# Seven pairs of experts instead of six in a mixture, with a pair last whose outputs come back through the matrix engine

## The chip, the cores and the metric

The kernel runs on one core of a Trainium2 chip as one launch. The metric is the device time of that launch in microseconds. The engines are TensorE (PE in the profile: matmuls; PEld: its weight loads), VectorE (DVE), ScalarE (ACT), GpSimd (POOL), and SyncE (SP), whose queue issues most of the transfers.

## The reference, cut to what matters

Two transformer blocks run one after the other on 512 tokens of width 1024, in float32. The first ends in a mixture of 32 experts, of which the router picks 4 for each token, and a gated addition of a second input `p`. That part is:

```python
def expert_block(args):
    xblk, e = args
    hg, hl = jnp.split(xblk @ w_gu[e] + b_gu[e], 2, axis=-1)
    hg = jnp.minimum(hg, SWIGLU_LIMIT)
    hl = jnp.clip(hl, -SWIGLU_LIMIT, SWIGLU_LIMIT)
    glu = hg * jax.nn.sigmoid(hg * SWIGLU_ALPHA)
    return ((hl + 1.0) * glu) @ w_down[e] + b_down[e]
...
y = (yb * row_gate[:, None]).astype(x2d.dtype)
return jnp.zeros((t + 1, d), x2d.dtype).at[row_tok].add(y)[:t]
...
h = DEEPNORM_ALPHA * x + ffn
h = h + jax.nn.sigmoid(h @ ple_gate_w[i]) * (p[i] @ ple_proj[i])
x = _layer_norm(h, ln2_g[i], ln2_b[i])
```

An expert's weights are 1024x2048 and 1024x1024 floats, 12.6 MB; the 32 of them are 403 MB, all of which is read.

## The kernel before, in words

The mixture is one stage, in which each engine runs its own instruction stream and they meet at semaphores. Its work is cut into **units**. A **single** is one expert with up to 128 tokens: its weights are split into two reduced-precision halves (`wh` on ScalarE, `wl` on VectorE), and each product is three matmuls (`wide_chunk`, L2632 to L2634). A **pair** is two experts with up to 64 tokens each, side by side in the 128 columns of the array, with plain float32 matmuls and no split (`pair_chunk`, L2651 and L2652). Experts are ranked by their number of tokens; the first `FEW` = 2 x `PAIRS` ranks, the smallest, go to the pairs. Tokens beyond an expert's room are counted in `over`; if there are any, `RestOfExperts` computes every expert again for the late tokens, with all 512 columns.

An expert's weights are 12 **chunks** of 1 MB (`CHUNKS`; a pair has 24). SP issues them in order (`chunk_in`, L2452) into 8 slots (`raw` and two in a borrowed tile, shown as `y` in the DMA rows); a pair has 8 more slots, `more_raw`, which lie over `wh` and `wl`. An issue waits until its slot is free: `w_low` counts chunks split, `used` chunks multiplied. The order of units is `s s p s s s p ... s s s`, 20 singles and 6 pairs: each turn of the loop in `all_units` is a single, a pair and two singles.

Around a unit, GpSimd gathers the rows of the next unit's tokens (L2511) and scatters the finished unit's outputs with addition into `y_rows` in memory (L2516), after ScalarE has weighted them by the gates (`weighted`, L2743). `kept` and `returned` order these.

After the last unit comes `Embedding` (`ple`). TensorE computes `p @ ple_proj` in 8 tiles (`embedded_tile`, L3166 to L3168, 48 matmuls), which needs `p` and the projection split by ScalarE (L3218, L3222) and VectorE (`vector_p` L3253, `vector_proj` L3257). Then `turn` (L3179) transposes the sums that SP has read back from `y_rows` (`sync_y`, L3152) once the last scatter has landed; VectorE adds them to `x` (L3270), and ScalarE and VectorE split `x` (L3240, L3273). Dummy matmuls stand between the transposes (`K.keep_busy`, L236). Then come 8 gate tiles (`tile`, L3192 to L3197, 24 matmuls each), each followed by a sigmoid on ScalarE (L3245), and the layer norm.

## Time and profile before

| | |
|---|---|
| time, median of 3 runs | 3280.78 us (3277.88 to 3282.35) |
| span of the profiled execution, first to last instruction | 3281.2 us |
| TensorE busy | 3121.0 us, 95% |
| VectorE, ScalarE, GpSimd busy | 2092.6, 1598.0, 211.7 us |
| moved by transfers | 600.37 MB, 183 GB/s over the whole span |

The page gives the span and no other time for the profiled execution, so sums are made against 3281.2 us, which lies 0.4 us above the median of the runs. Times in the rows are counted from the start of the span. The mixture stage reaches from about 477 to 1557 us. Matmuls overlap: a 128x512 matmul is shown as 0.39 us long while the next starts 0.23 us later, so the distance of the starts is what counts.

### The profile page before, as it was taken

How to read it: one execution, taken by the hardware profiler on the slowest of the kernel's cores; microseconds unless marked ns; L12 is line 12 of the kernel's file. 1: busy time of each engine (PE TensorE's matmuls, PEld its weight loads, DVE VectorE, ACT ScalarE, POOL GpSimd, SP SyncE). 2: the span in 40 equal slices, each digit the busy share in tenths (PEclk: the TensorE clock that was granted, in tenths of full speed). 3: DMA queues.
4: the chain of work that ended last, by engine and by line, in shares of the span. 5: the costliest groups of instructions: out<-in, count | busy, mean ns of one | idle time of the engine just before them, and what ended most of it. 6: DMA issues, size and time to landing. Idle time of an engine off the chain costs nothing. (4 is left out here: it accounts for less than half of the span.)

```text
span 3281.2 us, 48141 instructions
## 1 busy us (share of the span) xinstructions
PE 3121.0 (95%) x18751; PEld 2346.5 (72%) x18751; DVE 2092.6 (64%) x2561; ACT 1598.0 (49%) x1943; POOL 211.7 (6%) x202
## 2 busy tenths in 40 slices
PE   8998899999989999999999999999999999999998
PEld 6876567574747474848768777788877776778886
DVE  6745758484848484849478866666438876566544
ACT  4424336464646473737376355444226536444422
POOL 0000001121212121211000000000000000000000
PEclk9999999999999999999999999999999999999999
DMA  4113259999999999998122111222322211123331
GB/s 152 59 33 104 79 198 373 412 399 410 390 407 387 409 388 403 392 406 322 63 87 72 66 46 40 89 97 97 108 73 78 72 65 37 54 87 99 96 106 62
DMA packets 117708, 600.37 MB, mean 183 GB/s; under 512 B 19490, under 2 KB 23090, under 8 KB 67138
## 3 DMA queue, kind: packets, MB, share of 16 engines
q1 hardware_dynamic: 105442, 580.57, 46.6%
q0 software_dynamic: 12096, 17.40, 2.1%
q8 instruction: 122, 2.00, 0.2%
q14 instruction: 48, 0.39, 0.0%
HBM read 582.62 MB, written 27.33 MB: 186 GB/s over the span
## 5 line engine op out<-in xcount | busy, mean ns | idle before, releaser
L2823 DVE TENSOR_TENSOR wl<-raw,wh 128x2048 fp32r<-128x2048 f32 x174 | 397.1, 2288 | 69.8 <-ACT wh L2736 68.9
L2736 ACT ACTIVATE wh<-raw 128x2048 fp32r<-128x2048 f32 x174 | 333.5, 1917 | 134.3 <-PE pu L2634 62.4
L4740 ACT ACTIVATE w_high<-w_raw 128x1024 fp32r<-128x1024 f32 (+1 forms) x112 | 129.0, 1152 | 302.0 <-PE acc L4712 161.1
L2632 PE MATMUL pu<-wh,Xh 128*128 128x512 f32 x640 | 259.8, 406 | 16.2 <-DVE wl L2823 16.2
L4789 DVE TENSOR_TENSOR w_low<-w_raw,w_high 128x1024 fp32r<-128x1024 f32 (+1 forms) x112 | 150.0, 1339 | 180.4 <-PE ps L4670 95.1
L2633 PE MATMUL pu<-wl,Xh 128*128 128x512 f32 x640 | 253.1, 395 | 0.0
L2634 PE MATMUL pu<-wh,Xl 128*128 128x512 f32 x640 | 253.0, 395 | 0.0
L4692 PE MATMUL ps<-x_high,w_high 128*128 128x512 f32 x640 | 249.1, 389 | 0.0
L4693 PE MATMUL ps<-x_low,w_high 128*128 128x512 f32 x640 | 249.0, 389 | 0.0
L3537 PE MATMUL acc<-x_high,w_high 128*128 128x512 f32 x528 | 219.7, 416 | 1.5 <-ACT hq L3946 1.5
L3538 PE MATMUL acc<-x_low,w_high 128*128 128x512 f32 x528 | 207.5, 393 | 1.7 <-issue 1.7
L4670 PE MATMUL ps<-x_high,w_low 128*128 128x512 f32 x704 | 173.2, 389 | 0.5 <-DVE w_low L4789 0.5
L2632 PEld LDWEIGHTS pu<-wh,Xh 128*128 128x128 f32 x640 | 122.4, 191 | 45.7 <-DVE wl L2823 18.1
L2823 DVE TENSOR_TENSOR wl<-y,wh 128x2048 fp32r<-128x2048 f32 x66 | 150.9, 2287 | 3.3 <-ACT wh L2736 3.3
L4670 PEld LDWEIGHTS ps<-x_high,w_low 128*128 128x128 f32 x704 | 132.0, 188 | 28.7 <-DVE w_low L4789 1.4
L4214 DVE TENSOR_TENSOR w_low<-w_raw,w_high 128x1024 fp32r<-128x1024 f32 (+1 forms) x102 | 115.8, 1138 | 51.8 <-PE acc L3543 23.5
L2634 PEld LDWEIGHTS pu<-wh,Xl 128*128 128x128 f32 x640 | 122.4, 191 | 27.2
L2633 PEld LDWEIGHTS pu<-wl,Xh 128*128 128x128 f32 x640 | 122.7, 192 | 24.1
L4705 PE MATMUL acc<-h_high,w_high 128*128 128x512 f32 x352 | 137.2, 390 | 1.5 <-DVE h_low L4823 1.5
L4692 PEld LDWEIGHTS ps<-x_high,w_high 128*128 128x128 f32 x640 | 120.2, 188 | 25.4 <-DVE cv L4800 0.4
L4693 PEld LDWEIGHTS ps<-x_low,w_high 128*128 128x128 f32 x640 | 120.1, 188 | 24.9
L2736 ACT ACTIVATE wh<-y 128x2048 fp32r<-128x2048 f32 x66 | 126.8, 1922 | 21.7 <-DMA y<-in_exp_w 8.7
(920 smaller groups left out, 7208.9 us busy)
## 6 DMA issues: line engine op xcount, KB each, us to landing
raw<-in_exp_w SPq DMA_DIRECT2D x234, 1024.0 KB, 16.1
y<-in_exp_w SPq DMA_DIRECT2D x78, 1024.0 KB
more_raw<-in_exp_w SPq DMA_DIRECT2D x72, 1024.0 KB, 17.4
w_raw<-in_w_in SPq DMA_DIRECT2D x100, 512.0 KB, 3.4
w_raw<-in_w_up SPq DMA_DIRECT2D x80, 512.0 KB, 3.7
w_raw<-in_w_down SPq DMA_DIRECT2D x32, 704.0 KB, 4.0
w_raw<-in_w_out SPq DMA_DIRECT2D x32, 384.0 KB, 3.1
kv_raw<-in_w_mem_kv SPq DMA_DIRECT2D x16, 512.0 KB, 3.8
```

The costliest lines, as they stand in the source:

```text
L2632: nc.tensor.matmul(o, lh[:, k, :], wh[:, m % PARTS, c], start=(m >= 8 and kh == 0 and kk == 0), stop=False)
L2633: nc.tensor.matmul(o, lh[:, k, :], wl[:, m % PARTS, c], start=False, stop=False)
L2634: mm = nc.tensor.matmul(o, ll[:, k, :], wh[:, m % PARTS, c], start=False, stop=end)
L2736: nc.scalar.activation(wh[:, m % PARTS, :], piece, ACT.Copy).then_inc(w_high, 1)
L2823: nc.vector.tensor_tensor(wl[:, m % PARTS, :], slot_of(n, m)[0], wh[:, m % PARTS, :], ALU.subtract).then_inc(w_low, 1)
L3537: nc.tensor.matmul(o, wh[:, n % 3, c], high[:, k, :], start=(k == 0), stop=False)
L3538: nc.tensor.matmul(o, wh[:, n % 3, c], low[:, k, :], start=False, stop=False)
L4670: mm = nc.tensor.matmul(o, wl[:, u % 2, c], high[:, k, :], start=False, stop=(k == DT - 1))
L4692: nc.tensor.matmul(o, wh(u)[:, c], high[:, k, :], start=(k == 0), stop=False)
L4693: nc.tensor.matmul(o, wh(u)[:, c], low[:, k, :], start=False, stop=False)
L4705: nc.tensor.matmul(o, wh(u)[:, c], hh[:, f * PART + k, :], start=(f == 0 and k == 0), stop=False)
L4789: nc.vector.tensor_tensor(wl[:, u % 2, 0:width(u)], raw_of(u), wh(u), ALU.subtract).then_inc(low_ready, 1)
```

## The change

There are 7 pairs and 18 singles in the order `sssp` four times and `ssp` three times, so that the last unit is a pair (`ORDER`; `Unit` now works its counts out from its place). The last unit's outputs are not scattered to memory. ScalarE weights them into `y_parts`, rounded to reduced precision, and VectorE makes the remainder (`weighted_low`). VectorE also makes a matrix of zeros and ones that says to which token each row belongs (`place_back`). TensorE multiplies the two parts by it (`join`, 16 matmuls), which gives the outputs in the layout of `x`, and VectorE adds them (`take_joined`). The transposes of `y_rows` are moved ahead of `embedded_tile` and alternate with the joins, and the dummy matmuls between them are gone. SP reads `y_rows` when six chunks of the last pair are used and all earlier scatters have landed, before the projection and `p`. The splits of `p` and the projection on VectorE now come after the additions; the splits of `x` go beside `embedded_tile`. GpSimd's work after the last unit is gone. ScalarE weights the unit before a pair two places earlier. Four small memsets (`tile_starts`) are added at the stage's start.

```diff
-PAIRS = 6
+PAIRS = 7
 FEW, WIDE = 2 * PAIRS, EXPERTS - 2 * PAIRS
 UNITS = WIDE + PAIRS
 HALF = SLOTS // 2
+SCATTERS = WIDE + 2 * (PAIRS - 1)
+ORDER = 4 * "sssp" + 3 * "ssp"
+ROUND_FROM, ROUNDS, ROUND_UNITS, ROUND_WIDE, ROUND_PAIRS = 4, 3, 4, 3, 1
...
-        unit(a3, a4)
-    unit(Unit(UNITS - 1, WIDE - 1, EXPERTS - 2, one + (3 * one + two) * PAIRS + one, 1, PAIRS, PAIRS, 12, last=True), None)
+    def run(places, i=0):
+        for place in places:
+            unit(Unit(place, i), Unit(place + 1, i) if place + 1 < UNITS else None)
+
+    run(range(ROUND_FROM))
+    with eng.Fori(0, ROUNDS) as i:
+        run(range(ROUND_FROM, ROUND_FROM + ROUND_UNITS), i)
+    run(range(ROUND_FROM + ROUNDS * ROUND_UNITS, UNITS))
 
 
...
                 sp.wait_ge(saved, 16)
-                sp.wait_ge(w_low, (WIDE - 1) * CHUNKS + 7)
+                sp.wait_ge(scattered, SCATTERS * 16)
+                sp.wait_ge(used, (UNITS - 1) * CHUNKS + 6)
+                ple.sync_y(sp)
+                sp.wait_ge(used, (UNITS - 1) * CHUNKS + 10)
                 ple.sync_proj(sp)
-                sp.wait_ge(w_low, (WIDE - 1) * CHUNKS + 8)
                 ple.sync_p(sp)
-                rest.sync(sp, used)
-                sp.wait_ge(used, (UNITS - 1) * CHUNKS + 8)
-                for n in range(3):
-                    ple.sync_gate(sp, n)
-                sp.wait_ge(scattered, (UNITS + PAIRS) * 16)
-                ple.sync_y(sp)
-                for n in range(3, DT):
+                rest.sync(sp, joined_taken, DT)
+                for n in range(DT):
                     ple.sync_gate(sp, n)
 
             @block.gpsimd
@@ -2556,9 +2565,6 @@
                 pool.wait_ge(cleared, 2)
                 pool.wait_ge(kept, 16 * NT)
                 all_units(pool, unit)
-                scatter(Unit(UNITS, WIDE, 0, 0, 0, PAIRS, 0, 0))
-                pool.wait_ge(scattered, (UNITS + PAIRS) * 16)
-                pool.sem_inc(returned, 1)
 
             @block.tensor
             def _(pe):
...
+
+                def join(odd, k):
+
+                    if k == 0:
+                        pe.wait_ge(back_placed, 1)
+                        pe.wait_ge(y_low, 2)
+                    if k >= 2:
+                        pe.wait_ge(joined_taken, k - 1)
+                    c = slice(k * P, (k + 1) * P)
+                    nc.tensor.matmul(pd[:, k % 2, :], y_parts[:, odd, c], back_sel, start=True, stop=False)
+                    nc.tensor.matmul(pd[:, k % 2, :], y_parts[:, 1 - odd, c], back_sel, start=False, stop=True).then_inc(joined, 1)
 
...
-                rest.tensor(pe, y_ready)
+                for k in range(DT):
+                    ple.tensor_turn(pe, k)
+                    join((UNITS - 1) % 2, k)
+                rest.tensor(pe)
                 ple.tensor(pe)
 
...
-                def weighted(at, odd, d):
+                def weighted(at, odd, d, split):
                     act.wait_ge(used, at * CHUNKS + (11 + d))
                     if d == 0:
                         act.wait_ge(returned, at + 1)
                         act.wait_ge(paid, at * 2 + 2)
-                    nc.scalar.activation(y[:, odd, d * 512:(d + 1) * 512], pd[:, d, :], ACT.Copy, scale=gneg[:, odd:odd + 1]).then_inc(y_ready, 1)
+                    to = y_parts if split else y
+                    nc.scalar.activation(to[:, odd, d * 512:(d + 1) * 512], pd[:, d, :], ACT.Copy, scale=gneg[:, odd:odd + 1]).then_inc(y_ready, 1)
 
                 def gate(n, c):
                     act.wait_ge(used, n.at * CHUNKS + (4 * c + 2))
@@ -2773,16 +2794,17 @@
                                 turned_part(n.at - 1, 1, False)
                                 x_part(n, 0)
                                 x_part(n, 1)
-                            if m in (2, 3):
-                                weighted(n.at - 1, 1 - n.odd, m - 2)
+                            if m in ((0, 1) if n.pair else (2, 3)):
+                                weighted(n.at - 1, 1 - n.odd, m % 2, False)
                         if m in (5, 9):
                             gate(n, (m - 5) // 4)
                         if m == 8:
                             turned_part(n.at, 0, n.pair)
                     if n.pair:
...
-                        x_part(following, 0)
-                        x_part(following, 1)
+                        if not n.last:
+                            x_part(following, 0)
+                            x_part(following, 1)
 
                 nc.scalar.activation(rl[:, :].rearrange("p (j g e) -> p j g e", j=NT, g=4),
...
-                turned_part(UNITS - 1, 1, False)
+                for d in (0, 1):
+                    weighted(UNITS - 1, (UNITS - 1) % 2, d, True)
                 ple.scalar_p(act)
-                act.wait_ge(w_low, (WIDE - 1) * CHUNKS + 10)
                 ple.scalar_proj(act)
-                for d in (0, 1):
-                    weighted(UNITS - 1, 1, d)
+                act.wait_ge(joined_taken, DT)
                 rest.scalar(act)
...
+
+                def place_back(n):
+
+                    nc.vector.tensor_copy(back_row[:, 0:1], back[:, n.odd:n.odd + 1]).then_inc(back_rows, 1)
+                    dve.wait_ge(back_rows, 1)
+                    nc.vector.tensor_scalar(back_row[:, 1:1 + NT], tile_starts[:, :], back_row[:, 0:1], None, ALU.add).then_inc(back_rows, 1)
+                    dve.wait_ge(turned, n.at * 2 + 2)
+                    dve.wait_ge(back_rows, 2)
+                    nc.vector.tensor_tensor(back_sel.rearrange("p (j s) -> p j s", j=NT), K.c("iota").unsqueeze(1).to_broadcast([P, NT, P]),
+                                            back_row[:, 1:1 + NT].unsqueeze(2).to_broadcast([P, NT, P]), ALU.is_equal).then_inc(back_placed, 1)
+
+                def weighted_low(at, odd, d):
+                    c = slice(d * 512, (d + 1) * 512)
+                    if d == 0:
+                        dve.wait_ge(scattered, SCATTERS * 16)
+                    dve.wait_ge(y_ready, at * 2 + (d + 1))
+                    nc.vector.scalar_tensor_tensor(y_parts[:, 1 - odd, c], pd[:, d, :], gneg[:, odd:odd + 1], y_parts.bitcast(F32)[:, odd, c],
+                                                   ALU.mult, ALU.subtract).then_inc(y_low, 1)
+
+                def take_joined(k):
+                    dve.wait_ge(joined, k + 1)
+                    nc.vector.tensor_tensor(x[:, k, :], x[:, k, :], pd[:, k % 2, :], ALU.add).then_inc(joined_taken, 1)
 
                 def pay(at, odd, pair=False):
...
                             turned_low(n.wide, 0)
-                    if not n.last and not n.pair:
+                    if n.last:
+                        place_back(n)
+                    elif not n.pair:
...
+                for j in range(NT):
+                    step.go(nc.vector.memset(tile_starts[:, j:j + 1], -float(j * P)))
...
-                turned_low(WIDE - 1, 1)
+                for d in (0, 1):
+                    weighted_low(UNITS - 1, (UNITS - 1) % 2, d)
+                for k in range(DT + 1):
+                    if k < DT:
+                        ple.vector_turned(dve, k)
+                    if k:
+                        dve.wait_ge(ple.added, k)
+                        take_joined(k - 1)
                 ple.vector_p(dve)
                 ple.vector_proj(dve)
-                rest.vector(dve, used)
-                dve.wait_ge(used, UNITS * CHUNKS)
+                rest.vector(dve)
                 ple.vector(dve)
 
...
+    def tensor_turn(self, pe, k):
+        if k >= 3:
+            pe.wait_ge(self.added, k - 2)
+        for j in range(NT):
+            if k == 0:
+                pe.wait_ge(self.y_in[j], 16)
+            mm = self.nc.tensor.transpose(self.bank[k % 3][:, j * P:(j + 1) * P], self.yt[:, j, k * P:(k + 1) * P], self.K.c("ident"))
+        mm.then_inc(self.turned, 1)
...
-            if k:
-                K.keep_busy(norm.spare, 256)
-            if k >= 3:
-                pe.wait_ge(self.added, k - 2)
...
+            nc.scalar.activation(self.high[:, t, :], self.x[:, t, :], ACT.Copy).then_inc(self.x_split_h, 1)
             if t in (2, 5):
                 high_part(t // 3)
-        for k in range(DT):
-            act.wait_ge(self.added, k + 1)
-            nc.scalar.activation(self.high[:, k, :], self.x[:, k, :], ACT.Copy).then_inc(self.x_split_h, 1)
         for n in range(DT):
             act.wait_ge(self.product, n + 1)
...
+    def vector_turned(self, dve, k):
+        dve.wait_ge(self.turned, k + 1)
+        self.nc.vector.tensor_tensor(self.x[:, k, :], self.x[:, k, :], self.bank[k % 3], ALU.add).then_inc(self.added, 1)
+
...
-        low_part(0)
-        low_part(1)
         for k in range(DT):
-            dve.wait_ge(self.turned, k + 1)
-            nc.vector.tensor_tensor(x[:, k, :], x[:, k, :], self.bank[k % 3], ALU.add).then_inc(self.added, 1)
-            if k:
-                dve.wait_ge(self.x_split_h, k)
-                nc.vector.tensor_tensor(low[:, k - 1, :], x[:, k - 1, :], high[:, k - 1, :], ALU.subtract).then_inc(self.x_split_l, 1)
-        dve.wait_ge(self.x_split_h, DT)
-        nc.vector.tensor_tensor(low[:, DT - 1, :], x[:, DT - 1, :], high[:, DT - 1, :], ALU.subtract).then_inc(self.x_split_l, 1)
+            dve.wait_ge(self.x_split_h, k + 1)
+            nc.vector.tensor_tensor(low[:, k, :], x[:, k, :], high[:, k, :], ALU.subtract).then_inc(self.x_split_l, 1)
+            if k in (3, 6):
+                low_part(k // 3 - 1)
         for n in range(DT):
             dve.wait_ge(self.gate, n + 1)
             dve.wait_ge(self.e_taken, n + 1)
```

## Rows read from the trace of the kernel before

**Rows 1.** The page's part 2: the span in 40 equal slices, the transfers' rate.
```profile
GB/s 152 59 33 104 79 198 373 412 399 410 390 407 387 409 388 403 392 406 322 63 87 72 66 46 40 89 97 97 108 73 78 72 65 37 54 87 99 96 106 62
```

**Rows 2.** Busy time by stretches: a pair, and the two singles after the last pair.
```profile
core 0: us, PE busy (x) PEld busy (x) DVE busy (x) ACT busy (x) POOL busy (x), PEclk, DMA share, GB/s
...
574.00:621.00 47.00, 46.58 (x231) 15.96 (x229) 6.05 (x12) 6.51 (x10) 4.83 (x6) 1.00 1.01 411
...
1446.00:1522.00 76.00, 73.22 (x338) 59.16 (x335) 72.47 (x56) 62.23 (x48) 17.00 (x13) 0.98 1.02 409
```

**Rows 3.** TensorE's timeline (start, duration in us): openings of units 0, 1, 2, 7, 15, 23, 25.
```profile
500.44 0.51 PE L2604 MATMUL pu<-brow,ones 32*128 32x512 f32 x4 [0.86 <-DVE Xl L2842]
...
538.24 0.51 PE L2604 MATMUL pu<-brow,ones 32*128 32x512 f32 x4
...
574.58 0.64 PE L2601 MATMUL pu<-brow,ones 32*64 32x512 f32 x1
...
785.16 0.51 PE L2604 MATMUL pu<-brow,ones 32*128 32x512 f32 x4
...
1115.10 0.51 PE L2604 MATMUL pu<-brow,ones 32*128 32x512 f32 x4
...
1446.52 0.50 PE L2604 MATMUL pu<-brow,ones 32*128 32x512 f32 x4
...
1522.63 0.50 PE L2604 MATMUL pu<-brow,ones 32*128 32x512 f32 x4
```

**Rows 4.** The transfers' view from 1430 to 1458 us.
```profile
DMA packets 1607, 11.72 MB, mean 419 GB/s; under 512 B 176, under 2 KB 176, under 8 KB 176
```

**Rows 5.** Line 2452, issue to landing: from 500 to 560 us, then from 1100 to 1530.
```profile
DMA to landing us min/median/max: 4.9/7.2/9.6
...
DMA to landing us min/median/max: 10.8/16.5/29.0
```

**Rows 6.** TensorE at the sixth pair's last chunk and the single behind it.
```profile
1442.93 0.61 PE L2651 MATMUL pd<-more_raw,h 128*64 128x512 f32 x1 [1.32 <-issue]
...
1450.07 0.40 PE L2633 MATMUL pu<-wl,Xh 128*128 128x512 f32 x1
1450.30 0.39 PE L2634 MATMUL pu<-wh,Xl 128*128 128x512 f32 x1
...
1453.05 0.63 PE L2632 MATMUL pu<-wh,Xh 128*128 128x512 f32 x1
1453.48 0.63 PE L2633 MATMUL pu<-wl,Xh 128*128 128x512 f32 x1
```

**Rows 7.** TensorE behind the last unit: projection, transposes, first gate tile.
```profile
1557.70 0.47 PE L3166 MATMUL pu<-p_high,v_high 128*128 128x512 f32 x1
...
1568.45 0.39 PE L3168 MATMUL pu<-p_high,v_low 128*128 128x512 f32 x1
1569.96 0.33 PE L3179 MATMUL pu<-const,y_tokens 128*128 128x128 f32 x1 [1.11 <-DMA y_tokens<-y_rows]
...
1573.78 0.48 PE L3179 MATMUL pu<-const,y_tokens 128*128 128x128 f32 x1 [0.95 <-DMA y_tokens<-y_rows]
```

**Rows 8.** ScalarE in the same stretch.
```profile
1557.71 0.69 ACT L2743 ACTIVATE y<-pd,gneg 128x512 f32<-128x512 f32 x1 [2.03 <-PE pd L2634]
...
1568.88 0.60 ACT L3235 ACTIVATE e<-pu 128x512 f32<-128x512 f32 x1 [0.68 <-PE pu L3168]
...
1588.10 0.60 ACT L3245 ACTIVATE g<-pu 128x512 f32<-128x512 f32 x1 [3.38 <-PE pu L3197]
```

**Rows 9.** VectorE in the same stretch.
```profile
1551.72 1.22 DVE L3253 TENSOR_TENSOR p_low<-p_raw,p_high 128x1024 fp32r<-128x1024 f32 x1
1553.13 2.29 DVE L3257 TENSOR_TENSOR v_low<-v_raw,v_high 128x2048 fp32r<-128x2048 f32 x1 [0.19 <-ACT v_high L3222]
...
1578.58 0.68 DVE L3270 TENSOR_TENSOR x<-x,pu 128x512 f32<-128x512 f32 x1
1579.18 0.69 DVE L3273 TENSOR_TENSOR x_low<-x,x_high 128x512 fp32r<-128x512 f32 x1
```

More of the change, by code:

```diff
@@ L2305 @@
 HALF = SLOTS // 2
+SCATTERS = WIDE + 2 * (PAIRS - 1)
+ORDER = 4 * "sssp" + 3 * "ssp"
+ROUND_FROM, ROUNDS, ROUND_UNITS, ROUND_WIDE, ROUND_PAIRS = 4, 3, 4, 3, 1
 class Unit:
-    def __init__(self, at, wide, rank, bias, odd, pairs, turn, off, pair=False, behind=False, first=False, last=False):
-        self.at, self.wide, self.rank, self.bias, self.odd, self.pairs, self.turn, self.off, self.pair = at, wide, rank, bias, odd, pairs, turn, off, pair
-        self.behind, self.first, self.last = behind, first, last
@@ L2316, in all_units, with __init__ @@
-def all_units(eng, unit):
-    one, two = 64, 128
-    unit(Unit(0, 0, EXPERTS - 1, one, 0, 0, 0, 0, first=True), Unit(1, 1, FEW, 2 * one, 1, 0, 0, 12))
-    with eng.Fori(0, PAIRS) as i:
-        u, l, b = i * 4, i * 3, i * (3 * one + two)
-        a0 = Unit(u + 1, l + 1, l + FEW, b + 2 * one, 1, i, i, 12)
-        a1 = Unit(u + 2, l + 1, i * 2, b + (2 * one + two), 0, i, i, 24, pair=True)
-        a2 = Unit(u + 3, l + 2, l + (FEW + 1), b + (3 * one + two), 1, i + 1, i, 36, behind=True)
-        a3 = Unit(u + 4, l + 3, l + (FEW + 2), b + (4 * one + two), 0, i + 1, i, 48)
-        a4 = Unit(u + 5, l + 4, l + (FEW + 3), b + (5 * one + two), 1, i + 1, i, 60)
-        unit(a0, a1)
-        unit(a1, a2)
-        unit(a2, a3)
-        unit(a3, a4)
-    unit(Unit(UNITS - 1, WIDE - 1, EXPERTS - 2, one + (3 * one + two) * PAIRS + one, 1, PAIRS, PAIRS, 12, last=True), None)
+    def __init__(self, place, i=0):
+        before = ORDER[:place]
+        singles, self.pair = before.count("s"), ORDER[place] == "p"
+        self.first, self.last = place == 0, place == UNITS - 1
+        self.behind = not self.first and ORDER[place - 1] == "p"
+        self.odd, self.off, self.turn = place % 2, place * CHUNKS, i * (16 * ROUND_UNITS * CHUNKS // RAW)
+        self.at = i * ROUND_UNITS + place
+        self.wide = i * ROUND_WIDE + (singles - self.pair)
+        self.pairs = i * ROUND_PAIRS + before.count("p")
+        self.rank = EXPERTS - 1 if self.first else i * (2 * ROUND_PAIRS) + 2 * before.count("p") if self.pair else i * ROUND_WIDE + (FEW + singles - 1)
+        self.bias = i * (64 * ROUND_WIDE + 128 * ROUND_PAIRS) + (64 * (singles + (not self.pair)) + 128 * (before.count("p") + self.pair))
@@ L2361, in mixture @@
         vc = K.sb(ctx, "vc", [P, 512])
+        with ExitStack() as high:
+            y_parts = K.sb(high, "y_parts", [P, 2, D], F32R)
         y = K.sb(ctx, "y", [P, 2, D])
@@ L2373, in mixture @@
             sg = K.sb(held, "sg", [P, 512])
+            with ExitStack() as high:
+                hb_parts = K.sb(high, "hb_parts", [P, 2, 512], F32R)
             hb = K.sb(held, "hb", [P, 2, 512])
@@ L2424, in slot_of @@
                 where = raw[:, v, :] if v < HELD else spare_raw[:, v - HELD, :]
-                return where, loaded[v], n.turn * 96 + (16 * ((n.off + c) // RAW) + 16)
+                return where, loaded[v], n.turn + (16 * ((n.off + c) // RAW) + 16)
             def pair_slot(n, c):
@@ L2793, in _ @@
                 nc.scalar.activation(gpart[:, :, :, 0], ranked, ACT.Copy).then_inc(g_high, 1)
-                start = Unit(0, 0, EXPERTS - 1, 64, 0, 0, 0, 0, first=True)
+                start = Unit(0)
                 high_part(start, 0)
@@ L3169, in embedded_tile @@
             mm.then_inc(self.e_made, 1)
-        def turn(k):
-            if k:
-                K.keep_busy(norm.spare, 256)
-            if k >= 3:
-                pe.wait_ge(self.added, k - 2)
-            for j in range(NT):
-                if k == 0:
-                    pe.wait_ge(self.y_in[j], 16)
-                mm = nc.tensor.transpose(bank[k % 3][:, j * P:(j + 1) * P], self.yt[:, j, k * P:(k + 1) * P], K.c("ident"))
-            mm.then_inc(self.turned, 1)
         def tile(n):
@@ L3201, in tensor @@
             embedded_tile(t)
-        for k in range(DT):
-            turn(k)
         for n in range(DT):
```

22 lines of the change are left out of this document (11 added, 11 removed).

## The prediction

> **What bounds the kernel now.** The slices of the page come first, because they show which resource is full in the mixture stage. From the seventh slice to the eighteenth (about 490 to 1480 us) 373 to 412 GB/s flow, and nowhere else in the kernel more than 322 [rows 1]. The busy times by stretches say whether that is the limit. In a pair's 47 us ScalarE and VectorE are nearly idle; in the two singles after a pair TensorE, VectorE and ScalarE work for 73, 72 and 62 of 76 us; in both the transfers' share is 1.0 [rows 2]. So I looked at the distance from issue to landing. A chunk takes 4.9 us when the queue is nearly empty, which happens only under the first two singles; from 1100 us on it never takes under 10.8 us [rows 5], so four chunks or more are always outstanding, and the queue doesn't run dry. With no gather or scatter in the way 419 GB/s flow [rows 4]: 1.049 MB in 2.50 us.
>
> The starts of the units give the periods. From the second pair's end to the sixth's, 785.2 to 1446.5 us, four rounds of three singles and a pair take 165.3 us each [rows 3]. Their 60 chunks need 60 x 2.50 = 150.0; the other 15.3 us go to the gathers and scatters of four units, 3.8 us each. The transfers set the round, and each pair ends when its last weights do: TensorE begins the last chunk at 1442.93 after a wait and is done 3.6 us later [rows 6, 3]. Only the start, where eight slots fill before TensorE begins at 500.4, and the end, where three singles at TensorE's own pace follow the last pair, are outside this rule. The last single ends at 1557.7, and the outputs' way through memory comes behind it [rows 3, 7].
>
> **The change part by part.** I add up to the moment at which the first gate tile's product is taken by ScalarE, 1588.1 before [rows 8]. What follows is unchanged.
>
> *The start.* Two singles up to 574.6 as before; a third directly behind singles costs what the second did, 574.6 - 538.2 = 36.3 (36.4 with the unrounded start) [rows 3]: 610.9. The stretch from the first pair's start to the second pair's end is the same sequence as before, 785.2 - 574.6 = 210.6: 821.5. Two more `sssp` rounds, as from 785.2 to 1115.1, 329.9 [rows 3]: 1151.4.
>
> *Three rounds of `ssp`.* TensorE alone needs 76.1 for the two singles behind a pair (1522.6 - 1446.5) [rows 3] and 47 for a pair that doesn't wait [rows 2], 123; the queue needs 48 x 2.50 + 3 x 3.8 = 131.4. It sets the round: 394.2, so the last pair ends at T = 1545.6. If the 15.3 us go with bytes and not with units, the round is 165.3 x 48/60 = 132.2 and T = 1548.0; if gathers and scatters cost the queue nothing, TensorE's 123 would bind and T = 1520, which the period of 165.3 for 60 chunks excludes. I take 131.4, because the rate falls in the stretches where gathers run. Pairs and singles together do not need fewer bytes: all 384 chunks are still read, and one unit's gather and scatter are saved, which has paid for the third single at the start (36.3 against 33.8). So the advance of T, 1557.7 - 1545.6 = 12.1 us, comes almost wholly from having a unit last that follows its weights by 3.6 us in place of three that lag.
>
> *Coming back.* The last chunk lands at T - 3.6 = 1542.0. The four reads of `y_rows` stand behind it in SP's queue, and nothing of SP's stands between; they wait for scatters that have long landed. They come 1.27 us apart, (1573.78 - 1569.96)/3 [rows 7]: the fourth at 1547.1. In the meantime ScalarE weights the second half in 0.69 and VectorE makes its remainder, for which the trace has no row; the nearest VectorE operations of 128x512 take 0.68 to 0.69 [rows 8, 9]: 1547.1 too. With 0.4 for the last transposes, VectorE begins to add at 1547.5. It has 16 additions, one starting 0.60 behind the other [rows 9]. TensorE's part of each step, four transposes and two matmuls, is about 1.0 against VectorE's 1.2: VectorE sets it, 9.6 plus 0.6 for the first wait: 1557.7. Below, the joins can't be free; above, if TensorE's steps set the pace at half clock, a step takes 1.9 and the loop 5.6 more.
>
> *The projection.* VectorE turns to `p_low` and `v_low` only now. Before, they were covered by the last single; now nothing covers them, 1.22 + 2.29 = 3.5 [rows 9], and TensorE waits: 1561.2. The 48 matmuls take 1568.7 - 1557.7 = 11.0 [rows 7]: 1572.2. The copy of the last tile behind them costs 0.6 (the `e` row) [rows 8], and 0.5 because ScalarE now also splits `x` and two weight tiles there, about as much work as TensorE's: 1573.3. The first gate tile has 24 matmuls at 0.227, 5.5, and 0.2 until ScalarE has it: 1579.0. The splits of `x` on VectorE run beside this and are 3 us ahead of their use. The clock comes on top.
>
> *TensorE's clock.* Behind the sixth pair TensorE is idle while a single's first chunk is split, and soon after, matmuls that had started 0.23 apart start 0.43 apart [rows 6], 1.2 in place of 2.4 GHz. The slow stretch begins after 1450.3 and reaches to about 1453.9: 3.4 us, at half rate a loss of 1.7. The new wait for `v_low`, 1557.2 to 1561.2, is as long at least, and the dummy matmuls are gone, so I take the 1.7 in full: 1580.7. The Trainium skill (TensorE: Matmul & The Clock Gate, Part 1: The HAM clock gate) says that the throttled state is the default and activity alone releases it. By that rule the removal of the dummy matmuls speaks against the change, and the sum ends at 1580.7; without it, at 1579.0.
>
> *What costs nothing.* The four memsets run while VectorE waits for a TensorE product at the start; uncovered, under 0.3. `place_back` waits for the last transposes of the pair and has three chunks' time, some 11 us, before it is needed; uncovered, 0.9. GpSimd's last scatter goes, and nobody waits for it. The earlier `weighted` frees a bank sooner within a pair. The projection and `p` land within 5 us behind `y_rows`, and their ScalarE splits lie beside the additions; if `p` were late, 3 us.
>
> Sum: 1588.1 - 1580.7 = 7.4 us off 3281.2, which is 3273.8 against the profiled execution and 3273.4 against the median; rounded, 3273.5.
>
> **The rivals.**
>
> *The small transfers go with bytes (15%).* For it: rates hardly differ between a pair's stretch and the whole round. T is 2.4 later: 3275.9. With the joins at half clock for one stretch of 3.4 us, which costs another 1 to 2, it ends at 3277: no measurable change.
>
> *The queue runs dry behind each pair (9%).* This ends on the slow side. The last four chunks of a pair are issued only when the seventh and eighth chunk are multiplied. With one single fewer between pairs TensorE arrives with less in store. If the queue empties there, each of the three `ssp` rounds pays up to one landing from an empty queue, 4.9 [rows 5]: 14.7 in all, 3288. It takes away the whole gain from 2.5 us a round, and is slower by over 0.2% from 4.7. Against it: the shortest landing in the later rounds is 10.8 [rows 5], 5.9 above the empty queue's, so that more than two chunks' lead would have to go; and TensorE already waits for its last chunk in the old pairs [rows 6].
>
> *The end is lighter (14%).* The clock holds through the new wait and the joins overlap more, and the stream is a little quicker for having one unit less: 1.7 + 2 to 3, 3269.
>
> *The pairs overflow (1%).* The change doesn't do what it says if an expert of ranks 12 and 13 has more than 64 tokens, because `RestOfExperts` then runs: 32 experts with 192 matmuls each of at least 0.39 us, over 2 ms. Against it: counting the router's choices on the reference's inputs, the fourteenth smallest of the ranked experts has 63 tokens.
>
> **How the numbers follow.** The forecast has 61%, with its own range from 3270 to 3277: T is open by 2.4 us, the clock by 1.7, the loop by some 2. A change of 0.2%, 6.6 us, is about what a measurement of this kernel can tell from none; it ends at 3274.2, inside that range. So of the forecast's 61% two thirds are faster and one third the same. Faster: 0.41 + 0.14 = 0.55. Same: 0.20 + 0.15 and a little of the dry queue = 0.36. Slower: 0.09, the dry queue and the overflow. Two in ten may be left out: the dry queue's worst and half of the lightest end, so the range goes from 3268 to 3280.
>
> **What would show it.** In the profile after, the units' starts: third single near 574.6, the first pair near 611, pairs ending near 821, 1151, 1283, 1414 and 1546, with TensorE's waits inside the late pairs grown to about 8 us. Issue to landing never under 8 us after 700. Behind the last pair, transposes from about 1546, additions on VectorE without gaps until 1558, an idle TensorE of about 4 us before `embedded_tile`, and the first sigmoid of the gate tiles near 1581. I am wrong if the last pair ends later than 1549, if the loop of the joins takes 15 us in place of 10, or if the drop of the clock comes twice.

## The result, and the profile of the changed kernel

The changed kernel takes 3267.39 us (median of 4 runs, 3265.16 to 3268.45), the kernel before 3281.57 on the same chip: ratio 0.9949, 95% interval 0.9937 to 0.9962, so 12 to 21 us faster. That is a gain of 14 us where 7.4 were forecast, and 0.6 us under the low end of the range. The profiled span went from 3281.2 to 3266.0 us.

TensorE's timeline of the changed kernel, the rows that answer to [rows 3]: the first single, the second, the third, the first pair, then the single behind the first, second, fourth, fifth and sixth pair, and the last pair's last chunk (as in [rows 6]).

```profile
504.31 0.50 PE L2610 MATMUL pu<-brow,ones 32*128 32x512 f32 x4 [0.90 <-DVE Xl L2863]
...
542.11 0.51 PE L2610 MATMUL pu<-brow,ones 32*128 32x512 f32 x4
...
577.85 0.50 PE L2610 MATMUL pu<-brow,ones 32*128 32x512 f32 x4
...
614.30 0.64 PE L2607 MATMUL pu<-brow,ones 32*64 32x512 f32 x1
...
661.00 0.50 PE L2610 MATMUL pu<-brow,ones 32*128 32x512 f32 x4
...
823.52 0.50 PE L2610 MATMUL pu<-brow,ones 32*128 32x512 f32 x4
...
1150.39 0.51 PE L2610 MATMUL pu<-brow,ones 32*128 32x512 f32 x4
...
1280.28 0.51 PE L2610 MATMUL pu<-brow,ones 32*128 32x512 f32 x4
...
1409.57 0.51 PE L2610 MATMUL pu<-brow,ones 32*128 32x512 f32 x4
...
1534.67 0.61 PE L2668 MATMUL pd<-more_raw,h 128*64 128x512 f32 x1 [1.28 <-issue]
```

The forecast's moments were 821, 1151, 1283, 1414 and 1546. Counted from the first unit (504.3 here, 500.4 before), the second pair ends 1.9 us early, the fourth 4.9, the fifth 6.4, the sixth 8.5, and the last, at 1538.2, 11.3. The three `ssp` rounds take 129.9, 129.3 and 128.6 us, not 131.4; `sssp` takes 163.4 on the mean of the two between 823.52 and 1150.39, not 165.

VectorE behind the last pair (answers to [rows 9]): first and last additions of the loop, then the two remainders.

```profile
1539.98 0.69 DVE L3306 TENSOR_TENSOR x<-x,pu 128x512 f32<-128x512 f32 x1
...
1549.41 1.28 DVE L2908 TENSOR_TENSOR x<-x,pd 128x512 f32<-128x512 f32 x2
1550.60 1.22 DVE L3298 TENSOR_TENSOR p_low<-p_raw,p_high 128x1024 fp32r<-128x1024 f32 x1
1551.74 2.28 DVE L3302 TENSOR_TENSOR v_low<-v_raw,v_high 128x2048 fp32r<-128x2048 f32 x1
```

TensorE in the same stretch (to [rows 7]): the wait for `v_low`, and where the spacing of matmuls changes.

```profile
1554.17 0.77 PE L3226 MATMUL pu<-p_high,v_high 128*128 128x512 f32 x1 [4.63 <-DVE v_low L3302]
1554.73 0.63 PE L3227 MATMUL pu<-p_low,v_high 128*128 128x512 f32 x1
1555.16 0.63 PE L3228 MATMUL pu<-p_high,v_low 128*128 128x512 f32 x1
...
1560.23 0.40 PE L3228 MATMUL pu<-p_high,v_low 128*128 128x512 f32 x1
1560.46 0.40 PE L3226 MATMUL pu<-p_high,v_high 128*128 128x512 f32 x1
```

ScalarE (to [rows 8]): the last `e` tile and the first gate tile.

```profile
1568.61 0.59 ACT L3282 ACTIVATE e<-pu 128x512 f32<-128x512 f32 x1
...
1575.06 0.60 ACT L3290 ACTIVATE g<-pu 128x512 f32<-128x512 f32 x1 [5.34 <-PE pu L3246]
```

Measured from the last pair's end T, the steps came as forecast until the projection: first addition T + 1.8 (forecast 1.9), loop done T + 12.4 (12.1), `v_low` done T + 15.8 (15.6). Then matmuls start 0.43 us apart for nearly 6 us, and the gate tile comes at T + 36.9 instead of 35.1.

So the change of the span is made up thus: mixture from 1057.3 to 1033.9, 23.4 us off; tail (T to the first gate tile) from 30.4 to 36.9, 6.5 on; what lies ahead of the first unit 3.9 on, what lies behind the gate tile 1693.1 to 1691.0, 2.1 off. The last two can't be ascribed to the change as they stand: over the twelve further executions profiled below, the start lay between 501.3 and 504.3 (501.4 to 502.6 for the three with the old order) and the rear between 1690.2 and 1699.9. On the mean of all profiled executions the start is 503.3 with the new order and 501.5 with the old, so up to 1.8 us of it may be the change's; no run separates them. Two questions were left: why the stream is 11.3 us ahead of the forecast, and what the tail costs.

The packets gave the first clue. The transfers' view of 700 to 1480 us shows that more bytes flow in the same time (before, 399 GB/s, then after):

```profile
DMA packets 49853, 311.06 MB, mean 399 GB/s; under 512 B 10190, under 2 KB 10190, under 8 KB 13489
```

```profile
DMA packets 50605, 316.33 MB, mean 406 GB/s; under 512 B 10242, under 2 KB 10242, under 8 KB 13683
```

In the trace's packet records the time of a weight packet of 8192 bytes (one partition's part of a chunk) has another distribution, over 650 to 1480 us. The first two rows are the two kernels, the others are runs told further on. "Slots" is how far the weight slots of `raw` and `more_raw` begin behind a multiple of 512 bytes in a partition. It is worked out from the tiles' sizes, with 128 bytes as the remainder of the place from which they count; no run shows that place, and the distances between kernels don't depend on it. The mixture runs from its first unit to its last product, and the last column says for how many of the tail's us the granted clock was 1.2 GHz.

```
kernel           slots  packets at 309 ns  311 to 322 ns  mixture us  tail us  slow clock us
before           448    55.3%              37.8%          1057.3      30.4     3.4
after            0      93.5%               0.9%          1033.9      36.9     6.8
before_again     448    54.7%              38.5%          1056.3      32.0     6.8
before_pad64     0      92.6%               1.3%          1048.7      31.9     6.8
slots_pad64      0      92.9%               1.0%          1048.4      30.3     3.4
after_again      0      93.8%               0.7%          1033.9      36.9     6.8
after_pad256     256    93.3%               0.9%          1033.8      36.8     6.8
after_pad448     448    50.4%              43.7%          1040.2      35.4     3.4
after_pad32      32     47.5%              46.4%          1042.5      36.0     6.8
six_pairs_last   0      92.9%               1.0%          1042.6      35.9     6.8
```

The last two columns go together: with the old order the tail takes 30.4 and 30.3 us with 3.4 us of slow clock, 32.0 and 31.9 with 6.8; with the new one 35.4 with 3.4, and 35.9 to 36.9 with 6.8.

### The profile page after: what moved, and what is told of

It reads as the page before. It is cut to its first block and busy times, and to the rows that moved or that the text cites. A ratio compares the mean times of both kernels' runs of the same rounds, so it can differ in the third digit from the quotient of the medians.

```text
span 3266.0 us, 47097 instructions
## 1 busy us (share of the span) xinstructions
PE 3103.1 (95%) x18657; PEld 2307.2 (71%) x18657; DVE 2036.6 (62%) x2537; ACT 1545.2 (47%) x1909; POOL 202.9 (6%) x199
## 5 line engine op out<-in xcount | busy, mean ns | idle before, releaser
L2844 DVE TENSOR_TENSOR wl<-raw,wh 128x2048 fp32r<-128x2048 f32 x166 | 378.3, 2287 | 65.4 <-ACT wh L2756 64.4
L2756 ACT ACTIVATE wh<-raw 128x2048 fp32r<-128x2048 f32 x166 | 318.1, 1917 | 123.5 <-DMA raw<-in_exp_w 66.4
L4784 ACT ACTIVATE w_high<-w_raw 128x1024 fp32r<-128x1024 f32 (+1 forms) x112 | 129.0, 1152 | 302.6 <-PE acc L4756 161.2
L2649 PE MATMUL pu<-wh,Xh 128*128 128x512 f32 x576 | 233.4, 405 | 15.8 <-DVE wl L2844 15.8
L2651 PE MATMUL pu<-wh,Xl 128*128 128x512 f32 x576 | 227.9, 396 | 0.0
L2650 PE MATMUL pu<-wl,Xh 128*128 128x512 f32 x576 | 227.6, 395 | 0.0
L2649 PEld LDWEIGHTS pu<-wh,Xh 128*128 128x128 f32 x576 | 110.1, 191 | 42.5 <-DVE wl L2844 17.7
L4750 PE MATMUL acc<-h_low,w_high 128*128 128x512 f32 x352 | 137.0, 389 | 0.0
L3587 PE MATMUL acc<-x_high,w_low 128*128 128x512 f32 x528 | 133.7, 390 | 2.8 <-DVE w_low L4258 2.8
L2651 PEld LDWEIGHTS pu<-wh,Xl 128*128 128x128 f32 x576 | 110.0, 191 | 24.2
L3976 ACT ACTIVATE w_high<-w_raw 128x1024 fp32r<-128x1024 f32 (+1 forms) x101 | 99.1, 985 | 56.5 <-PE lev L3832 54.7
```

The lines of the kernel that those rows point to most:

```text
L2649: nc.tensor.matmul(o, lh[:, k, :], wh[:, m % PARTS, c], start=(m >= 8 and kh == 0 and kk == 0), stop=False)
L2650: nc.tensor.matmul(o, lh[:, k, :], wl[:, m % PARTS, c], start=False, stop=False)
L2651: mm = nc.tensor.matmul(o, ll[:, k, :], wh[:, m % PARTS, c], start=False, stop=end)
L2756: nc.scalar.activation(wh[:, m % PARTS, :], piece, ACT.Copy).then_inc(w_high, 1)
L2844: nc.vector.tensor_tensor(wl[:, m % PARTS, :], slot_of(n, m)[0], wh[:, m % PARTS, :], ALU.subtract).then_inc(w_low, 1)
```

## The experiments

**Both kernels once more**, unchanged.

> The kernel before, profiled once more, because the changed kernel's mixture rounds took 163.1 and 163.8 us where those of before took 164.8 to 165.7, and its whole way from the first unit to the last was 11 us shorter than my sum. Theory A (the change makes the stream quicker): the four rounds from the second pair's end to the sixth's again average 165.3, within 0.3, and the mixture from first unit to last again takes 1057. Rival B (one execution's stream differs from another's by 1%): the rounds average anything from 163 to 166, and the mixture takes 1046 to 1060.

> The changed kernel once more, profiled and timed. Theory A: from first unit to the last pair's end again 1034, within 2 us; rounds of three singles and a pair 163 to 164. Rival B: anything from 1034 to 1045. Both: 36 to 37 us from the last pair's end to the first sigmoid of the gate tiles; a ratio to before of 0.9945 to 0.9965.

Measured: the kernel before 3286.9 us in one run, beside 3284.62, the median of its 11 runs there; the changed kernel 3267.11, ratio 0.9948 (0.9930 to 0.9967). The mixture and its rounds from the second pair on repeat within 1 us, the packets' shares within 1%. Theory A holds in both, and the 11.3 us are not one execution's.

**Six pairs, a pair last.** What does the seventh pair bring?

```diff
-PAIRS = 7
+PAIRS = 6
-ORDER = 4 * "sssp" + 3 * "ssp"
-ROUND_FROM, ... = 4, 3, 4, 3, 1
+ORDER = 2 * "ssssp" + 4 * "sssp"
+ROUND_FROM, ... = 10, 3, 4, 3, 1
```

> The changed kernel with six pairs and twenty singles in place of seven and eighteen: twice four singles and a pair, then four times three singles and a pair. The last unit is still a pair and the tail is unchanged. Theory: the stream sets the time, and the gain lies in having a pair last; then the seventh pair buys only one unit's small transfers less, minus what the stream loses while four singles run at TensorE's pace: within 3 us of the changed kernel, 3267 to 3270. Rival: TensorE's load still counts, a pair in place of two singles takes 73 - 53 = 20 us off TensorE, and much of it shows: 3275 or more.

Measured: 3277.54 us, ratio 0.9975 (0.9964 to 0.9986). That is the rival's time and not the theory's. The mixture takes 1042.6 us, 8.7 more than with seven pairs. Its first pair ends 193.4 us after the first unit (697.44, below, and a start of 504.0) and has used 72 chunks; the changed kernel has used 60 after 156.7. The 12 chunks more cost 36.7 us, about TensorE's pace for a single (35.7), where the queue later needs 163.4/5 = 32.7: 4.0 us. The other 4.7 are spread over the rounds.

```profile
697.44 0.51 PE L2610 MATMUL pu<-brow,ones 32*128 32x512 f32 x4
...
892.52 0.51 PE L2610 MATMUL pu<-brow,ones 32*128 32x512 f32 x4
```

So TensorE's load shows at the start, as the rival had it, but for 4.0 us and not for most of 20. The forecast had no term for this: the seventh pair is over a third of the mixture's gain, while the rest of the change, a pair last with its tail, brings 1048.7 - 1042.6 = 6.1 us of mixture and costs 4.0 of tail (35.9 against 31.9), both against the kernel before with its slots moved (the next run).

**Only the 64 bytes.** The changed kernel has two new small tiles, `back_row` and `tile_starts`, of 32 bytes a partition each, ahead of nearly all of the mixture's tiles. I had costed them at nothing.

```diff
         back_right = K.sb(ctx, "back_right", [P, 1], I32)
+        pad = K.sb(ctx, "pad", [P, 16])
```

> The kernel before with one edit: a tile of 64 bytes per partition that nothing uses, where the changed kernel has its two new small tiles (32 bytes each), so that every later tile of the mixture, the weight slots among them, lies 64 bytes further on, as in the changed kernel. No instruction is added. Seen so far: of the stream's 8 KB packets 55% take 309 ns in the kernel before and 93% in every kernel that has the two small tiles. Theory (the place of the slots sets how long a packet takes to be written): about 93% of the packets at 309 ns, from one pair's end to the next 163.4 us and not 165.3, the mixture from its first weight unit to its last matmul about 1046 us instead of 1057, the whole about 9 to 11 us faster than the kernel before. Rival (the faster packets come from the changed order, loop or tail): 55% stay at 309 ns, 165.3 us from pair to pair, no change within 2 us.

Measured: 3279.22 us (11 runs; before 3284.09), ratio 0.9983 (0.9974 to 0.9993). Packets at 309 ns: 92.6%. Pair to pair 163.3 us on the mean of the last five, before 165.1. The mixture is 8.6 us shorter, with no instruction added; 11 had been expected. The first two singles, which go at TensorE's pace, take 74.1 us with the pad and without, so it is not that the engines work faster on the moved tiles. The transfers' view of the same window:

```profile
DMA packets 50328, 314.82 MB, mean 404 GB/s; under 512 B 10240, under 2 KB 10240, under 8 KB 13539
```

The gain of the whole, 4.9 us by the medians, is smaller than the mixture's 8.6 and than the 9 to 11 expected. Of its profiled execution 1.0 went at the start and 1.5 in the tail, where the clock was slow for 6.8 us and not 3.4; the interval reaches from 2.3 to 8.5 us.

**The shift undone, and two other shifts, in the changed kernel** (a pad of 448 bytes, as shown, or of 256 or 32, which is 64 or 8 in place of 112). The pad stands ahead of the two small tiles and not behind them, as the expectations have it; what comes later moves as far either way.

```diff
         back_right = K.sb(ctx, "back_right", [P, 1], I32)
+        pad = K.sb(ctx, "pad", [P, 112])
```

> The changed kernel with one edit: an unused tile of 448 bytes per partition behind its two new small tiles, so that with their 64 bytes the slots lie 512 bytes further on than in the kernel before, that is at the same remainder of 512, 256 and 128. Theory (the place of the slots): packets back to about 55% at 309 ns, the mixture about 10 to 12 us longer than the changed kernel's 1033.9, the whole 9 to 11 us slower than the changed kernel and so about 4 us faster than the kernel before. Rival (order, loop or tail): as the changed kernel, 14 to 15 us faster than the kernel before.

> The changed kernel with an unused tile of 256 bytes per partition behind its two new small tiles: the slots begin at a multiple of 256 that is not one of 512. Theory A (a start at a multiple of 128 is enough, as two of the eight slots, which lie 384 bytes past a multiple of 512 in every kernel, suggest: 91% of their packets take 309 ns in the changed kernel): as the changed kernel, 93% at 309 ns, 14 to 15 us faster than the kernel before. Theory B (it takes a multiple of 512): fewer packets at 309 ns and up to 10 us slower than the changed kernel. Rival (the place doesn't matter): as the changed kernel, but then the two other runs of this call show no effect either.

> The changed kernel with an unused tile of 32 bytes behind its two new small tiles: the slots of the ring lie 32 bytes past a multiple of 512, the smallest shift that the tiles' placing allows. Theory A (any place that is not a multiple of 128 is slow, more or less alike): about 55% of the packets at 309 ns, 5 to 8 us slower than the changed kernel. Theory B (it is a matter of 64 bytes, and 32 past one is worse than 64 past 128): under 55% at 309 ns and more than 8 us slower. Rival (only the start 448 past a multiple of 512 is slow): as the changed kernel.

Measured: 448 bytes, slots at the same remainder as before: 3274.15 us, ratio 0.9972 (0.9962 to 0.9982), 50.4% at 309 ns, mixture 6.3 us longer than the changed kernel's. The direction is the theory's, the size is not: 10 to 12 us of mixture had been expected. 256 bytes: 3266.66, ratio 0.9950 (0.9937 to 0.9964), on the same chip 7.5 us under the run with 448; mixture 1033.8, nothing lost: theory A, slots that differ by 256 bytes are alike. 32 bytes: 3277.98, ratio 0.9979 (0.9969 to 0.9989), 47.5% at 309 ns, mixture 8.6 us longer, a little worse than 448 and so nearer to theory B; that only 448 is slow is ruled out. The transfers' view at 448:

```profile
DMA packets 50300, 314.17 MB, mean 403 GB/s; under 512 B 10201, under 2 KB 10201, under 8 KB 13642
```

**Only the weight tiles shifted**, in the kernel before (the tiles laid over them later move along).

```diff
+            pad = K.sb(held, "pad", [P, 16])
             with ExitStack() as parts:
                 wh = K.sb(parts, "wh", [P, PARTS, CW], F32R)
...
+            pad = K.sb(held, "pad", [P, 16])
             self.yt = yt = K.sb(held, "y_tokens", [P, NT, D])
```

> The kernel before, with the unused 64 bytes only ahead of the weight tiles (the parts and the weight slots; the embedding's tiles that later lie over them move along), while the gathered rows, the activations and the outputs stay where they were. Theory (the weight slots' own place sets their packets' time): as the run with the 64 bytes further ahead, about 93% of the 8 KB packets at 309 ns, 163.4 us from pair to pair, 3 to 9 us faster than the kernel before. Rival (the place of another tile, such as the one that gathers write, disturbs the transfers): 55% at 309 ns and no change.

Measured: 3279.79 us, ratio 0.9987 (0.9977 to 0.9998), 92.9% at 309 ns, mixture 1048.4. The theory holds: it is the weight tiles' place and not that of the gathered rows or the activations. The tiles of the split halves, `wh` and `wl`, share the room of `more_raw` and move with it; no run tells them apart.

**Dummy matmuls in the tail**, five between the last join and the projection of the changed kernel.

```diff
+                for _ in range(5):
+                    K.keep_busy(pu[:, 0, :], 512)
                 rest.tensor(pe)
                 ple.tensor(pe)
```

> The changed kernel with five dummy matmuls of 512 columns, about 0.86 us each at full clock, behind the last join, where TensorE waits 4.6 us for the projection's low part and the clock then stands at 0.5 from 1553.3 to 1560.2. If the wait causes the drop, the clock stays at 1.0, the projection's 48 matmuls take 11.0 in place of 14.3 us, and the time falls by 3.4 us. Rival: the drop comes from the thin work of transposes and joins ahead of the wait, and at least one slow stretch stays: 0 to 2 us.

Measured: 3265.22 us, ratio 0.9940 (0.9922 to 0.9957); tail 34.1, 2.8 less. The clock stays up, as the theory has it; the gain is 2.8 us in the trace and not 3.4. Busy time by stretches (the number behind the five busy times is PEclk, the granted clock), the changed kernel and this one:

```profile
1548.00:1553.00 5.00, 1.50 (x8) 0.73 (x6) 4.94 (x7) 0.00 (x0) 0.00 (x0) 1.00 0.02 5
1553.00:1560.00 7.00, 5.83 (x14) 4.61 (x15) 1.71 (x2) 1.45 (x3) 0.00 (x0) 0.52 0.01 2
```

```profile
1548.00:1553.00 5.00, 4.97 (x17) 2.41 (x15) 4.93 (x6) 0.00 (x0) 0.00 (x0) 1.00 0.02 5
1553.00:1560.00 7.00, 6.65 (x29) 5.11 (x28) 2.69 (x4) 3.97 (x7) 0.00 (x0) 1.00 0.01 2
```

TensorE was busy for 1.50 of the 5 us ahead of the drop to 1.2 GHz in the one and for 4.97 in the other, where the clock stays at 2.4 GHz. By the medians, 3265.22 against 3267.11, the gain is within the intervals; the trace shows it.

**One bank for transposes and joins**, so that VectorE adds a tile to `x` once.

```diff
-            mm = self.nc.tensor.transpose(self.bank[k % 3][...], self.yt[...], self.K.c("ident"))
+            mm = self.nc.tensor.matmul(self.bank[k % 3][...], self.yt[...], self.K.c("ident"),
+                                       start=(j == 0), stop=False, is_transpose=True, ...)
...
-                    nc.tensor.matmul(pd[:, k % 2, :], y_parts[:, odd, c], back_sel, start=True, stop=False)
+                    nc.tensor.matmul(ple.bank[k % 3], y_parts[:, odd, c], back_sel, start=False, stop=False, ...)
...
-                for k in range(DT + 1):
-                    if k < DT:
-                        ple.vector_turned(dve, k)
-                    if k:
-                        dve.wait_ge(ple.added, k)
-                        take_joined(k - 1)
+                for k in range(DT):
+                    take_joined(k)
```

> The changed kernel with one edit in the tail: a tile's four transposes of y_tokens and its two one-hot products are accumulated in one bank, and VectorE adds that bank to x once, so 8 additions where the changed kernel has 16. Theory (the stretch behind the last pair is set by VectorE's additions at 0.60 us each, then p_low and v_low): the last addition ends near 1545.5 and not 1550.6, p_low and v_low behind it near 1549, the first sigmoid of the gate tiles 32 us behind the last matmul of the mixture where the changed kernel has 36.9; about 5 us faster than the changed kernel. Rival (TensorE's own transposes and products, some 1.2 us for a tile, set the loop, or p_high and v_high are late): at most 2 us.

Measured: 3261.86 us, ratio 0.9938 (0.9924 to 0.9951), tail 33.5. VectorE's rows:

```profile
1540.54 0.69 DVE L2906 TENSOR_TENSOR x<-x,pu 128x512 f32<-128x512 f32 x1 [0.88 <-PE pu L2625]
1541.45 0.69 DVE L2906 TENSOR_TENSOR x<-x,pu 128x512 f32<-128x512 f32 x1 [0.22 <-PE pu L2625]
...
1546.87 0.69 DVE L2906 TENSOR_TENSOR x<-x,pu 128x512 f32<-128x512 f32 x1 [0.22 <-PE pu L2625]
1547.47 1.22 DVE L3293 TENSOR_TENSOR p_low<-p_raw,p_high 128x1024 fp32r<-128x1024 f32 x1
```

Between theory and rival: half the additions are gone, but now each waits 0.22 for TensorE, whose four transposes and two products take 0.90 a tile. The loop ends at T + 9.5 and not T + 12.4, 2.9 us sooner and not 5; the tail is 3.4 shorter. Its clock still falls, for 6.8 us from 1549.3.

**The same, fed:** `v_low` in quarters, and the five dummy matmuls.

```diff
-        self.nc.vector.tensor_tensor(self.v_low[:, :, :], ...).then_inc(self.v_split_l, 1)
+        for t in range(0, DT, 2):
+            self.nc.vector.tensor_tensor(self.v_low[:, t:t + 2, :], ...).then_inc(self.v_split_l, 1)
```

> As one_bank, with two more edits: v_low is made in four quarters, so that the projection starts behind the first (0.6 us) and not behind the whole (2.3 us), and five products of 512 columns that nothing uses stand between the last join and the projection. Theory: 1.7 us for the quarters and up to 2.8 us for the clock that stays up (what the same five products gave in the changed kernel), so 2 to 4.5 us faster than one_bank and 7 to 9 us faster than the changed kernel. Rival (with the shorter loop the clock doesn't fall at all, and the five products stand in the way): no faster than one_bank, or up to 1 us slower.

Measured: 3259.65 us (3257.29 to 3261.59), ratio 0.9928 (0.9915 to 0.9942), tail 31.0, 2.5 less than with one bank alone, and no slow stretch in it. That is the low half of the theory's 2 to 4.5 us. The rival is out, since with one bank alone the clock did fall. This kernel has the lowest median here, 23 us under the kernel before on its chip, and by the ratios some 7 under the changed one; the intervals of the two runs with one bank overlap.

**The outputs back through memory**, with seven pairs and a pair last.

```diff
+                pool.wait_ge(y_ready, UNITS * 2)
+                scatter_rows(back[0:HALF, o:o + 1], o)
+                pool.wait_ge(scattered, (SCATTERS + 1) * 16)
+                scatter_rows(back_right[:, :], o)
...
-                for k in range(DT):
-                    ple.tensor_turn(pe, k)
-                    join((UNITS - 1) % 2, k)
```

> Seven pairs and a pair last as in the changed kernel, but its outputs go back as everywhere else: two scatters that add into y_rows one after the other, y_rows read, transposes behind the projection as in the kernel before; no one-hot products and 8 additions of x and not 16. Theory (the round trip lies beside the projection, whose 11 us it needs anyway): the first sigmoid of the gate tiles 31 to 34 us behind the last matmul of the mixture (the kernel before 30.4 and 32.0, the changed kernel 36.9), so 3 to 5 us faster than the changed kernel. Rival (two scatters in turn and 2 MB of y_rows cost more than the loop of joins): 38 us or more, the changed kernel's one-hot products are worth their place.

The extract leaves out that `embedded_tile` stands ahead of the transposes again, and the dummy matmuls between these are back.

Measured: 3265.18 us, ratio 0.9947 (0.9934 to 0.9961), tail 35.9: within 1 us of the one-hot tail, between theory and rival. GpSimd's two scatters, and TensorE's last wait for the rows:

```profile
1537.13 1.44 POOL L2526 DMA_INDIRECT y_rows<-y,back  x1 [50.42 <-ACT y L2770]
1542.73 1.56 POOL L2526 DMA_INDIRECT y_rows<-y,back_right  x1 [4.15 <-DMA y_rows<-y,back]
```

```profile
1558.09 0.33 PE L3225 MATMUL pu<-const,y_tokens 128*128 128x128 f32 x1 [0.94 <-DMA y_tokens<-y_rows]
```

A scatter takes 5.6 us from issue to issue of the next, two of them and the read last until 1558.1, T + 22.7; the projection covers all but TensorE's three waits for them, 0.21, 0.92 and 0.94 us. The one-hot products, as written in the change, buy nothing; in one bank and fed, they do.

## Why the prediction was half right

- *Start and singles:* right. The third single came 35.7 and the pair 36.4 us behind the one before it (forecast 36.3).
- *The rounds, the step that failed:* "the queue needs 48 x 2.50 + 3 x 3.8 = 131.4 ... so the last pair ends at T = 1545.6". That the queue sets the round was right, and it never ran dry: the shortest issue to landing after 700 us is 10.8 us, as before (line L2464, issue to landing, from 700 to 1530 us, below). Its pace was taken from the kernel before and held for a property of the stream. It was partly one of the weight tiles' place: with the slots back at 448 the mixture takes 1040.2 us where 1045.2 were forecast and 1033.9 measured, so 6.3 of the missing 11.3 us are the 64 bytes. The two tiles stood in the diff, and the sum has no term for them, not even an open one.

```profile
DMA to landing us min/median/max: 10.8/16.5/29.5
```

- *The other 5.0 us* are a mis-sized term. With the slots at 448 the fourth pair ends 2.0 us ahead of the forecast's distance from the start, and the three `ssp` rounds take 131.3, 130.3 and 129.6, together 3.0 less than 394.2. By the same 2.50 a chunk, a unit's small transfers cost 3.5 us there and not 3.8. Why is not shown, so this part of the cause stays open; the rounds of the kernel before grow from 163.9 to 165.7 us, and I had taken the mean of the last four of five.
- *"Almost wholly from having a unit last":* wrong. By the runs, the mixture's 23.4 us are 8.6 from the slots, 6.1 from the pair last with the rest of the change, and 8.7 from the seventh pair, if the steps are taken in this order; taken last, the slots are worth 6.3. I had seen the third single at the start as a repayment, not the saved fourth one.
- *The tail:* 1.8 us longer than forecast, 36.9 against 35.1, and 1.1 of it is the clock. It stays at 1.2 GHz for 6.8 us, 1553.3 to 1560.2, not 3.4, which costs 2.8 by the run with dummy matmuls, not 1.7. The direction of the rule that the prediction takes from the Trainium skill (TensorE: Matmul & The Clock Gate, Part 1: The HAM clock gate) is borne out: the drop follows a stretch with TensorE busy 1.50 of 5 us, and goes when it is kept busy. The other 0.7 us lie in small steps on both sides of `v_low`. "The drop comes twice" was named as a way to be wrong; it came once, twice as long.
- *The rivals:* a queue running dry is not seen. If the small transfers went with bytes, a round of `ssp` would be 48/60 of 163.4 us, 130.7; the three take 129.3 on the mean. "The end is lighter" came nearest in time (3269). The quicker stream that it named came, and larger than it had it; the clock that it wanted held fell.
- *The signs:* the waits inside the late pairs grew less than said. The last three pairs take 53.3, 52.8 and 52.1 us where one that doesn't wait takes 47, so the wait is 5 to 6 us and not 8, which is the quicker stream again.
- *The total* looks nearer than its parts. The sum missed the span by 7.8 us, and this is made up of 11.3 too much in the mixture, 1.8 and 3.9 too little in the tail and at the start, and 2.1 too much behind the gate tile (with rounding).

## What to carry to other kernels

When a kernel is bound by its weight stream, look at where its slots begin; a small tile declared ahead of them moves them, and here that was worth 0.6 to 0.8% of the stream's time. A small tile belongs in the sum of a change, or at least among its open terms. Having last the unit whose weights are used as they land shortened the stream by 6.1 us and lengthened the tail by 4.0, so both belong in the sum. Singles at the start, where TensorE and not the queue sets the pace, should be few: the fourth cost 4.0 us. In a tail where one engine idles, first halve the other's operations and feed the idle one: that brought 5.9 us here, the choice between memory and products 1.0.

## What the runs showed of the hardware

In the kernels whose slots of `raw` and `more_raw` begin at 0 or 256 past a multiple of 512, 92.6 to 93.8% of the stream's packets of 8192 bytes take 309 ns. In those where they begin at 32 or 448 it is 47.5 to 55.3%, and nearly all of the difference is at 311 to 322 ns. In the mixture this is worth 8.6, 8.9, 6.3 and 8.6 us in four pairs of kernels that have the same instructions and differ in where tiles lie (in the second pair it is the weight tiles and the embedding's, in the others all tiles behind the pad).

A packet's own start doesn't settle its time. Slots 6 and 7 of the ring are in another tile, which lies at 384 in every kernel. A chunk has 16 landings in the trace; if each is taken for one of the 16 DMA engines, they tell how many engines are at a chunk at any time. Where at least 13 are at chunks of these two slots, 88.6% of the packets take 309 ns in the changed kernel and 89.3% with the pad of 256, but 60.3% in the kernel before, 47.7% with the pad of 448 and 44.3% with 32. Three engines of 16 at other chunks are too few to make this difference. So slots in a slow place go with slow packets in a slot beside them in the stream too, whose place has not changed. By what path is not shown.

In the kernels with a fast stream all slots lie a multiple of 128 bytes from each other, and in those with a slow one `raw` and `more_raw` lie 64 or 32 bytes off this; 64 bytes were tried only as 448.

The Trainium skill (DMA: Bandwidth & Descriptors, How a descriptor splits into AXI transactions) gives multiples of 256 bytes as the starts at which a transfer splits evenly. In the changed kernel the slots at 384 and those at 0 are both fast, and only one of these can be such a multiple wherever the tiles count from; that speaks against 256 as the bound for these writes. That unaligned starts cost extra agrees.
